# The first block of the token mixer's tail in a transformer trunk: heads and norms two to a slot

## The reference

```python
def conformer_conv(u, w, b, ln_w, ln_b, grid):
    ...
    return jax.nn.silu(layernorm(z, ln_w, ln_b))

def gla_output(o, r, gn_w):
    ...
    o = o * lax.rsqrt(jnp.mean(o * o, axis=-1, keepdims=True) + EPS)
    o = o.reshape(B, L, H * DV) * gn_w.astype(jnp.float32)
    return (o * jax.nn.silu(r.astype(jnp.float32))).astype(r.dtype)

def token_mixer(h, hc, ...):
    ...
    y = jnp.concatenate([conformer_conv(conf_u, ...), gla_output(o_lat, r, gla_gn_w),
                         short_conv(sc_u, sc_w, sc_b)], axis=-1) @ w_out
```

## Time and profile before

| | |
|---|---|
| median of 3 runs | 2190.05 us (2189.19 to 2193.42) |
| the profiled execution's own time | 2188.92 us |
| its span, first to last instruction | 2187.2 us |
| PE busy | 2087.8 us, 95% of the span |
| DVE busy | 1370.8 us, 63% |
| ACT busy | 992.4 us, 45% |
| mean granted TensorE clock | 0.977 of full speed |

### The profile page before, as it was taken

The page is one execution under the profiler, slowest core; times in us unless marked ns, Lnnn a source line. Parts: engine busy times, 40 slices in busy tenths (PEclk is TensorE's granted clock), DMA queues, the critical chain, the costliest instruction groups (busy, mean ns, idle before and its releaser), DMA issues. The chain is left out here.

```text
span 2187.2 us, 34697 instructions
## 1 busy us (share of the span) xinstructions
PE 2087.8 (95%) x13389; PEld 1826.1 (83%) x13389; DVE 1370.8 (63%) x2081; ACT 992.4 (45%) x1616; POOL 280.9 (13%) x355
## 2 busy tenths in 40 slices
PE   6999999999999799996899999999999999999994
PEld 4778888788777588884799999999999999999993
DVE  3663648995984667757555656556565565655656
ACT  5923554344631444421444544445444454444544
POOL 0000000000001011020011122111221112211120
PEclk9999999999999899997799999999999999999997
DMA  7473333343337665356347666576665765657655
GB/s 254 152 255 117 105 104 98 124 123 95 100 106 233 210 200 192 133 196 252 116 181 263 211 201 216 184 263 211 200 216 183 265 211 199 216 183 266 211 195 219
DMA packets 188283, 407.92 MB, mean 187 GB/s; under 512 B 15956, under 2 KB 53396, under 8 KB 187300
## 3 DMA queue, kind: packets, MB, share of 16 engines
q1 hardware_dynamic: 162212, 318.36, 42.0%
q0 software_dynamic: 25984, 88.39, 12.5%
HBM read 329.59 MB, written 77.12 MB: 186 GB/s over the span
## 5 line engine op out<-in xcount | busy, mean ns | idle before, releaser
L55 PE MATMUL bh<-xt_hi,shi 128*128 128x256 f32 x2048 | 572.4, 280 | 1.8 <-DVE xt_lo L2327 1.4
L56 PE MATMUL bh<-xt_lo,shi 128*128 128x256 f32 x2048 | 572.5, 280 | 0.0
L57 PE MATMUL bh<-xt_hi,slo 128*128 128x256 f32 x2048 | 572.4, 279 | 0.0
L2311 DVE TENSOR_TENSOR slo<-raw,shi 128x1024 fp32r<-128x1024 f32 x384 | 455.9, 1222 | 162.4 <-ACT shi L2225 157.9
L2225 ACT ACTIVATE shi<-raw 128x1024 fp32r<-128x1024 f32 x384 | 389.4, 1052 | 130.3 <-PE eby L57 125.7
L55 PEld LDWEIGHTS bh<-xt_hi,shi 128*128 128x128 f32 x2048 | 386.4, 189 | 2.9 <-DVE xt_lo L2327 1.8
L56 PEld LDWEIGHTS bh<-xt_lo,shi 128*128 128x128 f32 x2048 | 386.3, 189 | 0.6
L57 PEld LDWEIGHTS bh<-xt_hi,slo 128*128 128x128 f32 x2048 | 386.3, 189 | 0.0
L55 PE MATMUL bank<-h_hi,whi 128*128 128x512 f32 x704 | 283.6, 403 | 1.3 <-DVE wlo L709 1.3
L57 PE MATMUL bank<-h_hi,wlo 128*128 128x512 f32 x704 | 275.6, 391 | 0.0
L56 PE MATMUL bank<-h_lo,whi 128*128 128x512 f32 x704 | 275.4, 391 | 0.0
(11 more groups left out here) (332 smaller groups left out, 3134.9 us busy)
## 6 DMA issues: line engine op xcount, KB each, us to landing
raw<-in_exp_w_dram SPq DMA_DIRECT2D x96, 2048.0 KB, 11.1
uT<-stage POOLq DMA_DIRECT2D x72, 256.0 KB, 2.7
xb<-in_ada_w_dram SPq DMA_DIRECT2D x24, 512.0 KB, 5.5
wraw<-in_w_in_dram SPq DMA_DIRECT2D x22, 512.0 KB, 5.2
adaw<-in_ada_w_dram SPq DMA_DIRECT2D x8, 1024.0 KB, 10.0
xb<-in_x_dram SPq DMA_DIRECT2D x16, 512.0 KB, 4.4
xt<-in_x_dram POOLq DMA_DIRECT2D x16, 512.0 KB, 5.7
x2d<-xt POOLq DMA_DIRECT2D x16, 512.0 KB, 2.9
```

Of the source, the lines that this page charges most:

```text
L55: nc.tensor.matmul(out, w_hi, x_hi, start=start, stop=False)
L56: nc.tensor.matmul(out, w_hi, x_lo, start=False, stop=False)
L57: return nc.tensor.matmul(out, w_lo, x_hi, start=False, stop=stop)
L2311: nc.vector.tensor_tensor(item_dst(slo, n), item_src(n), item_dst(shi, n), ALU.subtract).then_inc(S["w_lo_ready"], 1)
```

## The change

Only the mix of block 0 and the order of the weight split change; the blocks 1 to 3 keep their schedule.

- TensorE does two heads and two norms in one slot. So that a pair needs no wait between its halves, the second of each pair writes another PSUM bank: `inter_bank` is `bt` or `bi`, and `norm_bank` is `bl` or `bn`. The waits for the earlier reader of the bank go back accordingly. Slot 3 has the mean and heads 0, 1; slot 4 the spread and heads 2, 3; slots 5 and 6 two norms each.
- ScalarE: four squares and the first root in slot 4; two squares, two roots and the Silu in slot 5; two weight rows and two roots in slot 6; two weight rows in slot 7. The last four weight rows come behind `cat_hi(0)`.
- VectorE follows in the same order, with its last four weight rows behind `cat_lo(0)`.
- SP: queries 2 and 3 are issued in slots 3 and 4 (before 5 and 6), gates 2 and 3 in slot 7 (before 8).

```diff
+        def inter_bank(i):
+            return bt if i < HEADS and i % 2 else bi
+
+        def norm_bank(i):
+            return bl if i < HEADS and i % 2 else bn
...
+            if r == 3:
+                query_in(sp, 2)
             if r == 4:
                 stages_done(sp, 4)
                 short_in(sp, 0)
+                query_in(sp, 3)
             if r == 5:
-                query_in(sp, 2)
                 short_in(sp, 1)
-            if r == 6:
-                query_in(sp, 3)
-            if r == 8:
+            if r == 7:
                 gate_in(sp, 2)
                 gate_in(sp, 3)
...
-            wait(pe, "added", i)
+            wait(pe, "added", i if n else i - 1)
...
-            wait(pe, "log_ready", 5 * n + 1 + h if h else 5 * n)
+            wait(pe, "log_ready", (5 * n + 1 + h if h else 5 * n) if n else (h if h >= 2 else 0))
...
         def tensor_ahead(pe, r):
             if r == 3:
-                done(pe, "u_read", "forward_ready", "k_read", "o_read")
+                done(pe, "u_read", "forward_ready", "k_read", "o_read", "a_ready")
                 pe.wait_ge(S["ones_set"], 1)
-            if 3 <= r < 9:
-                pe_mix(pe, 0, r - 3)
+                pe_mean(pe, 0)
+                pe_inter(pe, 0)
+                pe_inter(pe, 1)
+            if r == 4:
+                pe_spread(pe, 0)
+                pe_inter(pe, 2)
+                pe_inter(pe, 3)
+            if r in (5, 6):
+                pe_norm(pe, 2 * (r - 5))
+                pe_norm(pe, 2 * (r - 5) + 1)
...
         def scalar_ahead(act, r):
             if r == 3:
                 nc.scalar.preload_act_table_set("natural_log_exp_and_others")
-            if 3 <= r < 9:
-                act_mix(act, 0, r - 3)
-            if 6 <= r < 9:
-                w_high(act, 2 * (r - 6))
-                w_high(act, 2 * (r - 6) + 1)
+            if r == 4:
+                act_square(act, 0, 0)
+                act_square(act, 0, 1)
+                act_square(act, 0, 2)
+                act_square(act, 0, 3)
+                act_root(act, 0, 0)
+            if r == 5:
+                act_square(act, 0, 4)
+                act_square(act, 0, 5)
+                act_root(act, 0, 1)
+                act_root(act, 0, 2)
+                act_silu(act, 0)
+            if r == 6:
+                w_high(act, 0)
+                w_high(act, 1)
+                act_root(act, 0, 3)
+                act_root(act, 0, 4)
+            if r == 7:
+                w_high(act, 2)
+                w_high(act, 3)
...
-            for k in range(6, 8):
-                act_mix(act, 0, k)
-                w_high(act, k)
             done(act, "multiplied")
             act.sem_inc(S["left"], 1)
             cat_hi(0)
+            for k in range(4, 8):
+                w_high(act, k)
...
         def vector_ahead(dve, r):
-            if 3 <= r < 9:
-                dve_mix(dve, 0, r - 3)
-            if 6 <= r < 9:
-                w_low(dve, 2 * (r - 6))
-                w_low(dve, 2 * (r - 6) + 1)
+            if r == 4:
+                dve_centre(dve, 0)
+                dve_add(dve, 0)
+                dve_add(dve, 1)
+            if r == 5:
+                dve_add(dve, 2)
+                dve_add(dve, 3)
+                dve_short(dve, 0)
+            if r == 6:
+                dve_scale_conv(dve, 0)
+                dve_gate(dve, 0)
+                dve_gate(dve, 1)
+                dve_short(dve, 1)
+                w_low(dve, 0)
+                w_low(dve, 1)
+            if r == 7:
+                dve_gate(dve, 2)
+                dve_gate(dve, 3)
+                w_low(dve, 2)
+                w_low(dve, 3)
```

More of the change, by code:

```diff
@@ L1325, in pe_inter @@
             pe.wait_ge(S[f"query_loaded{i % 2}"], 16 * (i // 2 + 1))
-            wait(pe, "added", i)
+            wait(pe, "added", i if n else i - 1)
             for j in range(TILES):
-                last = nc.tensor.matmul(bi[:, j * P:(j + 1) * P], v.state[h][:, TILES * n + j + 1, :],
+                last = nc.tensor.matmul(inter_bank(i)[:, j * P:(j + 1) * P], v.state[h][:, TILES * n + j + 1, :],
                                         qp[i % 2][:, j * P:(j + 1) * P], start=True, stop=True)
@@ L1334, in pe_norm @@
             pe.wait_ge(S["squares_ready"], 6 * n + 3 + h)
-            wait(pe, "log_ready", 5 * n + 1 + h if h else 5 * n)
-            nc.tensor.matmul(bn[:, :], ones[:, :], sq[h % 2][:, :], start=True, stop=True
+            wait(pe, "log_ready", (5 * n + 1 + h if h else 5 * n) if n else (h if h >= 2 else 0))
+            nc.tensor.matmul(norm_bank(i)[:, :], ones[:, :], sq[h % 2][:, :], start=True, stop=True
                              ).then_inc(S["squares_summed"], 1)
@@ L1391, in tensor_body @@
             pe.sem_inc(S["left"], 1)
-            for k in range(6, 8):
-                pe_mix(pe, 0, k)
             n_gate = 0
@@ L1439, in act_root @@
             wait(act, "scaled", i - 1)
-            nc.scalar.activation(rs[i % 2][:, :], (bn if r else bm)[:, :], ACT.Ln, bias=v.epsc[:, :],
+            nc.scalar.activation(rs[i % 2][:, :], (norm_bank(HEADS * n + r - 1) if r else bm)[:, :], ACT.Ln, bias=v.epsc[:, :],
                                  scale=1.0 / (DV if r else DCONF)).then_inc(S["log_ready"], 1)
@@ L1546, in dve_add @@
             o = cat[n % 2][:, 2 + h, :]
-            nc.vector.tensor_tensor(o, o, bi[:, :], ALU.add).then_inc(S["added"], 1)
+            nc.vector.tensor_tensor(o, o, inter_bank(i)[:, :], ALU.add).then_inc(S["added"], 1)
         def dve_scale_conv(dve, n):
@@ L1654, in normalise @@
                                         ).then_inc(S["aff_ready"], 1)
-            for k in range(6, 8):
-                dve_mix(dve, 0, k)
-                w_low(dve, k)
             dve.sem_inc(S["left"], 1)
             cat_lo(0)
+            for k in range(4, 8):
+                w_low(dve, k)
             for q in range(NQ + 8):
```

## The result

The changed kernel takes 2197.68 us (median of 8 runs, 2196.04 to 2200.27) against 2190.56 for the kernel before, measured beside it (8 runs). The ratio is 1.0036, 95% interval 1.0027 to 1.0045: slower by 7.1 us by the medians, 5.9 to 9.9 by the interval. The forecast was 2195.4, in a range of 2190.5 to 2198.8.

A forecast was written before the change was run, and what follows sets the result against it. TensorE matmul throughput bounds the kernel (busy 95%). A later block 1 mean, +3.2, and half clock, +2.2, sum to +5.4 us: profiled 2188.92 becomes 2194.3, the median 2195.4; range 2190.5 to 2198.8.

The forecast's parts named there:

- main chain: Block 1's conformer rows, queued on SP behind the last projected tile's store, make TensorE wait before pe_mean(1): +3.2 us.
- The reason I gave for the store's landing: Last projection store shares the pipe with weight load, broadcast and other stores, 4.45 MB; lands 741.0 instead of 736.2.
- E96: End of projection unit 96 on TensorE: 713.4 before, forecast 717.1 because inter(3) waits 1.9 us for the fourth query.
- The clock behind the second hole: After the new wait before block 1's mean, 4.5 us of TensorE matmuls at half clock: +2.2 us, bounds 0 to 3.4.
- A: Rival: the hole before the output projection simply shrinks, multiply(0) starts 4.9 us earlier and the stream goes on: 2185.2; 6%.
- B: Rival: transfers at the seam stay about where they are, inter(3) doesn't wait: +1.2 to +3.4 us, 2191.3 to 2193.5; 33%.
- D: Rival: all transfers at the seam late and a long slow clock: +5.2 + 3.4 = +8.6 us, 2198.7; 11%.
- C: The forecast itself, late block 1 mean plus half clock behind it: +4 to +7 us, 2194.0 to 2197.0; 50%.
- Free edits: In block 0's mix, extra semaphore waits and a pair's second bank cost nothing; VectorE keeps the same instructions, reordered.

The follow-up runs named there:

- the run with the queries first: Changed kernel with the fourth query issued directly behind the third, ahead of three short-convolution rows; 1.0028 of the kernel before, +6.4 us.
- the last version: Changed kernel with queries, second weight load and block 1's loads issued earlier, plus two more weight rows split behind the first tile; 0.9972 of the kernel before.

## Why the prediction was right

**The mechanism was right in its main chain.** The loads of block 1 stand behind the last store and hold `pe_mean(1)`: a wait of 9.6 us was measured where 7 to 8 was forecast, and moving them takes it away. The last store lands 24.0 us after unit 96 ends (forecast 23.9), the weight load is issued 10.6 after (10.7), the last store 17.3 (17.8). `multiply(0)` starts 19.4 after unit 96 ends, where 20.2 was forecast, and the hole before it is 4.8 us, where 5.5 was. One reading was wrong and did no harm: between the end of the last unit and `cat_hi(0)` the kernel before splits four weight rows and not two (two at 730.24, two at 737.60); the sum itself takes four copies off the chain.

**The reason I gave for the store's landing was right as a whole and off in its parts.** I took the sum of all bytes in the pipe. Its order mattered: taking the broadcast away brought 3.3 us. Taking the larger load away brought 1.1, which is less than the same store differs between two executions with no load beside it (5.4 and 7.3 us).

**The term that was mis-sized is E96.** I had 717.1, 20.0 us after t0; it was 23.1, beyond my upper bound of 718 (20.9 after t0). The query was issued on time (4.8 after t0), but took 10.0 us and not 8.8: 1.4 us with the restart of the inter. Its own matmuls went slower, 0.4. And I held the clock to stay up over this hole. It fell: unit 96 took 6.7 us and not 5.44, 1.3 us that stand in no line of the forecast. (Unit 95, also directly behind an inter but at full clock, took 5.58, so some 1.2 of it is the clock.) From the store to the mean it was 12.6 and not 12.2. Together 3.6: the mean is +6.9 against before and not +3.2, and outside my bounds of -0.6 to +5.2.

**The clock behind the second hole** cost 3.5 us at half speed, 1.7 (forecast 2.2). The sum is 8.6; the last output matmuls of the two traces stand 8.7 apart against t0, and nothing of it was absorbed up to there. From there to the end the changed kernel's execution was 1.4 us shorter (1200.1 against 1201.5 us), so from t0 to the end it lost 7.3. That stretch lies between 1199.6 and 1201.5 us in all twelve traces, whatever the kernel, so I take the 1.4 as chance and not as part of the change. The medians give 7.1 (5.9 to 9.9) and the forecast was +5.3 on the median. That the total came out closer than the mean of block 1 is luck: the clock cost 0.5 less than I had, and the rest of the difference is the variation between executions.

**The rivals.** A, the hole simply shrinks, needed the rows before 745.6; they came at about 758. B needed the query in time; it was 3.2 us late. D's long slow clock (3.4 us lost) wasn't reached here, but the run with the queries first lost 2.6. The result lies just above C (+4 to +7), on the side of D, by a late unit 96 and not by the clock.

**Free edits.** In the changed kernel the second banks of a pair cost nothing; the only wait at a pair's second half is the query's. VectorE's order cost nothing either; only with two rows ahead of the tile did ScalarE wait for it, 0.7 us.

## What to carry to other kernels

Before a hole on the bound engine is closed, look at the next thing that engine needs behind the hole, and how long before its use that lands: here 1.3 us of slack capped a hole worth 13.5 us. When evictions are delayed to do other work first, everything queued behind their stores is delayed too, on the store queue and on every queue that waits for the stores; loads that don't read what is stored belong ahead of that wait. A reordering that lost 7 us gained 7 us once three DMA issues had been put in their right places, so a loss is a reason to look for the queue and not yet to drop the idea.

## What the runs showed of the hardware

The granted clock fell in short holes, and not after the same time. It fell about 3.6 us after TensorE stopped in the 3.2 us query wait (just behind the restart), 2.3 us after in the hole of the last version and in the earlier trace rows, 5.1 us after ahead of the output projection in the changed kernel (at about 741.7). After a restart it stayed at half for 3.5 us before the mean of block 1 in the changed kernel, 4.5 in the earlier trace rows, and with the queries first 5.3 at the mean and 6.0 at the first output matmul (735.90 to about 741.9). Half of that time is lost work: 1.7 us at the query wait, 1.7 to 2.6 in the other cases. So the price of a hole of 3 to 11 us in this kernel was the hole and 1.7 to 2.6 us more; the 3.0 at the first output matmul lay inside the wait for the mean and cost nothing. That the clock falls between bursts that wait for transfers is what the Trainium skill describes ("TensorE: Matmul & The Clock Gate", HAM oscillation — how this bites in real kernels), and the trace agrees.

A store of 0.26 MB took 3.2 us to land beside a 2 MB weight load issued 6.7 us before it on the same queue, 5.4 to 7.3 beside a 1.5 MB broadcast on another queue, 6.6 to 9.4 beside both. The broadcast hurt it more than the larger load ahead of it in its own queue, which I had not expected; but that load was nearly through (it landed 2.0 us after the store was issued), so the two are not compared at equal age.
